# A group norm's last two steps, moved two half steps later in a hand-written order of events

## The reference

```
o   = retention(rotary(q), rotary(k), v)        # 512 x 128 of one head
mu  = mean(o, -1);  var = mean((o - mu)^2, -1)
o_r = (o - mu) * rsqrt(var + 1e-5) * silu(g_r)   # head group norm and gate
```

## Time and profile before

| | |
|---|---|
| median of three runs | 1423.04 us |
| the profiled execution | 1422.83 us, span 1420.7 us |
| PE busy | 1374.6 us, 97% of the span |
| DVE busy | 1037.6 us, 73% |
| ACT busy | 748.3 us, 53% |
| POOL busy | 114.0 us, 8% |
| granted TensorE clock, mean | 0.993 of 2.4 GHz |

### The profile page before, as it was taken

The page is one execution under the profiler, slowest core; times in us unless marked ns, Lnnn a source line. Parts: engine busy times, 40 slices in busy tenths (PEclk is TensorE's granted clock), DMA queues, the critical chain, the costliest instruction groups (busy, mean ns, idle before and its releaser), DMA issues.

```text
span 1420.7 us, 22721 instructions
## 1 busy us (share of the span) xinstructions
PE 1374.6 (97%) x8648; PEld 1230.9 (87%) x8648; DVE 1037.6 (73%) x1115; ACT 748.3 (53%) x1013; POOL 114.0 (8%) x164
## 2 busy tenths in 40 slices
PE   6999999999999999999989999989999999999997
PEld 6999999999787788767768888789999999978786
DVE  6977887788789874657664344687788777779796
ACT  6545544544685552667763323554454445448663
POOL 0000000001420000333220000000000000024100
PEclk9999999999999999999999999999999999999999
DMA  6323332337997655212113345232333233399974
GB/s 200 93 87 118 118 101 76 118 118 207 249 225 253 237 192 133 75 45 60 46 45 88 90 148 177 75 121 75 117 118 104 82 109 118 116 285 210 247 258 142
DMA packets 161638, 194.47 MB, mean 137 GB/s; under 512 B 6064, under 2 KB 116912, under 8 KB 161456
## 3 DMA queue, kind: packets, MB, share of 16 engines
q1 hardware_dynamic: 147808, 166.74, 36.5%
q0 software_dynamic: 13056, 25.17, 9.7%
q10 hardware_dynamic: 720, 1.84, 0.3%
HBM read 187.43 MB, written 6.29 MB: 136 GB/s over the span
## 4 chain that ended last, share of the span: by engine, by line
PE 74%; DVE 10%; DMA 9%; ACT 3%; issue 2%; POOL 2%; SPq 0%; DVEq 0%; ACTq 0%; POOLq 0%
PE ps L700 15%; PE ps L702 15%; PE ps L703 15%; DMA w_raw<-w_ffn_down 5%; PE ps L666 5%; PE ps L668 5%; PE ps L667 5%; DMA d_sum<-w_ffn_down 2%; PE ps L800 2%; PE ps L801 2%; PE ps L802 2%; DVE w_lo L1826 2%; PE ps L673 1%; PE ps L674 1%; PE ps L675 1%
## 5 line engine op out<-in xcount | busy, mean ns | idle before, releaser
L700 PE MATMUL ps<-s_hi,w_hi 128*128 128x256 f32 x960 | 273.0, 284 | 4.8 <-DVE w_lo L1641 4.8
L702 PE MATMUL ps<-s_lo,w_hi 128*128 128x256 f32 x960 | 272.7, 284 | 0.0
L703 PE MATMUL ps<-s_hi,w_lo 128*128 128x256 f32 x960 | 272.7, 284 | 0.0
L700 PE MATMUL ps<-a_hi,w_hi 128*128 128x256 f32 x816 | 233.1, 286 | 3.0 <-DVE a_lo L1596 3.0
L702 PE MATMUL ps<-a_lo,w_hi 128*128 128x256 f32 x816 | 232.5, 285 | 0.0
L703 PE MATMUL ps<-a_hi,w_lo 128*128 128x256 f32 x816 | 232.4, 285 | 0.0
L1173 ACT ACTIVATE w_hi<-w_sum 128x1024 fp32r<-128x1024 f32 x120 | 124.0, 1057 | 174.9 <-DVE w_sum L1668 80.4
L700 PEld LDWEIGHTS ps<-s_hi,w_hi 128*128 128x128 f32 x960 | 185.5, 193 | 5.1 <-DVE w_lo L1641 5.1
L800 PE MATMUL ps<-w_hi,l_hi 128*128 128x512 f32 x448 | 175.9, 393 | 11.9 <-DVE w_lo L1826 11.9
L702 PEld LDWEIGHTS ps<-s_lo,w_hi 128*128 128x128 f32 x960 | 185.5, 193 | 0.0
L703 PEld LDWEIGHTS ps<-s_hi,w_lo 128*128 128x128 f32 x960 | 185.4, 193 | 0.0
(11 more groups left out here) (203 smaller groups left out, 2577.7 us busy)
## 6 DMA issues: line engine op xcount, KB each, us to landing
w_raw<-w_ffn_down SPq DMA_DIRECT2D x80, 512.0 KB, 5.1
w_raw<-w_ffn_gate SPq DMA_DIRECT2D x64, 512.0 KB, 4.8
w_raw<-w_ffn_up SPq DMA_DIRECT2D x64, 512.0 KB, 5.0
d_sum<-w_ffn_down POOLq DMA_DIRECT2D x48, 512.0 KB, 13.1
w_raw<-w_in SPq DMA_DIRECT2D x44, 512.0 KB, 4.0
d_sum<-w_ffn_down SPq DMA_DIRECT2D x16, 512.0 KB, 9.3
x_mid<-x_tok SPq DMA_DIRECT2D x8, 512.0 KB, 4.9
x_tok<-x_mid SPq DMA_DIRECT2D x8, 512.0 KB, 7.3
```

The lines of the kernel that those rows point to most:

```text
L700: pe.matmul(o, wh, hi[:, k, :], start=first and f == 0 and k == 0, stop=False, skip_group_check=True)
L702: pe.matmul(o, wh, lo[:, k, :], start=False, stop=False, skip_group_check=True)
L703: mm = pe.matmul(o, wl, hi[:, k, :], start=False, stop=last and k == KH - 1, skip_group_check=True)
```

## The change

One line: `gn_e` stands at r = 9 instead of 7, `gn_f` at r = 11 instead of 9.

```diff
     per_pair = 12
-    gn_at = {3: "a", 5: "d", 7: "e", 9: "f"}
+    gn_at = {3: "a", 5: "d", 9: "e", 11: "f"}
     groups = []
```

## The result

The changed kernel took 1425.18 us (median of 19 runs, 1422.08 to 1427.71); the kernel before took 1422.10 us in the 19 runs beside it (1420.32 to 1424.22). The ratio is 1.0022, 95% interval 1.0016 to 1.0029: 3.1 us slower, between 2.3 and 4.1. The time lies inside the range on record and 0.5 us over the predicted time. That it comes so near is luck in part: the three runs shown beforehand (1423.04) lay 0.9 us over the median of the many. The difference from before is nearly twice the forecast 1.7 us, and close to what the first rival gave (1.7 + 1.7).

A forecast was written before the change was run, and what follows sets the result against it. PE, busy 97% of the span, was taken to bound the kernel. Gain 0, DVE's queue 1.52 us and POOL 0.14 sum to +1.66 us: 1424.7 us, own range 1424.0 to 1425.4, 8 in 10 1421.4 to 1427.0.

The forecast's parts named there:

- the first rival: The stall in pair 1 brings the granted clock down, +1.7 us more, 1426.4 us; chance 0.17.
- What the change removes: ACT in pair 1: the last attention tile's Exp starts some 2.5 us earlier, but PE had no gap; gain 0.
- The walk through DVE's queue: Pair 1: the reciprocal starts 6.5 us later, DVE's idle cover is used up, sp_lo and PE's matmul come 1.52 us late.
- POOL's share: Pair 1: POOL's masks and two copies fall beside DVE's w_lo and add 0.14 us; by the skill's rule 0.34 us.
- Pairs 2 and 3, the last norm: Pair 2 has 2 us of slack, pair 3 no following attention tile, the last norm's order is unchanged; cost 0.
- The clock: Behind pair 1's new hole of 1.5 to 1.9 us the granted clock most likely stays up; chance of a fall 0.17.
- The third rival: Everything behind 657 us shifts 1.7 us and the clock's dip behind the hole at 720 goes: 1423.0 us; chance 0.08.

The follow-up runs named there:

- the w_lo kernel: The full change, but in pair 1 DVE's weight split w_lo for unit 14 stands behind the softplus split, not ahead of sp_lo; 1424.14 us, ratio 1.0010.
- the kernel with two more products: The full change with two more products (0.72 us each) on DVE behind the reciprocal, in pair 1 alone; 1426.91 us, ratio 1.0034.

## Why the prediction was right in its mechanism and short in its size

**What the change removes: gain 0.** Right. The Exp came early in the change and in the kernel with the root at 8, and neither is faster than before.

**The walk through DVE's queue: 1.52 us, with POOL 1.66.** Right, place and size. PE's sp_lo matmul came 1.65 us late in the first trace. That the queue is the cause is shown by its dose, in the traces: 1.14 us taken out removed the wait for sp_lo, 1.45 us put in cost 1.44 more. That it starts with the Copy ahead of the root was in the walk too, and the root at r = 8, ahead of that Copy, cost nothing.

**POOL's share.** The sum was right, one term not. The w_lo beside POOL's copies took its usual 1.22 us and sp_lo lost 0.08 us (0.57 against 0.49), so 0.14 was too much and the 0.34 us worked out by the Trainium skill's rule was not there. What waited was POOL:

```profile
660.37 1.52 POOL L2146 COPY cum<-sp 128x128 f32<-128x128 f32 x2
```

Two copies that took 0.53 us together in the trace of before took 1.52 here. The first took its usual 0.29 us; the second, begun 0.08 us behind w_lo, took 1.29 and ended 0.16 us behind w_lo's end. The Trainium skill ("SBUF — State Buffer", the two separate sides) has a lock between the two engines that the first to start holds for a whole instruction; for w_lo and the second copy the trace agrees. For the first copy it shows no wait: w_lo began 0.14 us before that copy's end and still took 1.22 us. I had let DVE be the one that waits. The root again started 1.30 us behind the start of its table load (649.38 to 650.68): the further 1.38 us of drain that the Trainium skill has ("ScalarE: Activation LUTs", section on what ACT_TABLE_LOAD costs) were absent in the changed kernel too.

**Pairs 2 and 3, the last norm: 0.** Right: the kernel with all but pair 1 moved is at 1.0002. In pair 2 the sp_lo matmul had no wait.

**The clock: a chance of 0.17 for its fall, and nothing in the sum.** This is the step that failed. The working compared the new hole with two old ones, 1.34 us (clock stayed at 1.00) and 3.04 us (fell), and took the nearer. The nearer row was one execution. In the ten traces here and before that still have the hole of 1.34 us at 622, the clock falls behind it in three (the changed kernel, all but pair 1, and the w_lo kernel) and not in seven; behind the new hole of 1.4 to 2.8 us it falls in four of four. Nor does length alone decide: a hole of 1.66 us near 484 stood in the trace of before itself, with the clock at 1.00 behind it. So the cost of the change is 1.65 + 1.68 us when the clock falls. The mean over the runs agrees: the granted clock averaged over the span was 0.9914 in 19 runs of the change and 0.9927 in 56 runs of before, unrounded 0.0012 less, and 0.0012 of 1425 us is 1.7 us, the loss of about one fall more per execution. The same difference is 1.9 us for the kernel with two more products and 0.9 us for pair 1 alone, so the size of this part is known only roughly. The median's difference of 3.1 us (2.3 to 4.1) agrees with the first rival's 1.66 + 1.7.

**The third rival, a fall given back later,** is not borne out as it stands: the clock fell behind the hole at 720 in every trace of these sets that has it whole. Further on, something is given back in single executions. The trace of before has the clock down for 10.2 us in all between 915 and 965 us; the four traces with the new hole have it down there for 3.4 us or not at all. But so has that of all but pair 1 (3.4 us), without that hole, so these traces can't say that the hole brings it about. This is why single traces mustn't be compared by their ends: the kernel with two more products had the shortest span (1421.1 us) of the first set's traces and the longest median.

**What stays open.** Why a hole of 1.34 us at 622 brings the clock down in three of ten executions, one of 1.39 us or more at 660 in four of four, and one of up to 1.70 us near 484 in none of thirteen. Something beside the length of the hole counts, what PE does around it or when in an execution it falls; no run here separates that. Open too is the gap of up to 1.48 us at the start of the heads stage in some executions.

## What to carry to other kernels

A step moved later in a list that several engines share is free on an engine only as long as that engine reaches its next deadline with idle time to spare; walk that engine's queue from the moved instruction to the next one that the bounding engine needs, with start-to-start times, and look for the event that the moved step now stands behind (here a copy that waits for filling). And price a new hole in TensorE's work above its length, with the fall of the clock as a case of its own: here a microsecond and a half cost three, since the clock fell behind it, while a hole of the same length elsewhere in the same kernel brought no fall. The gain lay where TensorE already waited, in what stands ahead of the instruction that it waits for and in filling dealt to the step with the longest chain.

## What the runs showed of the hardware

- A hole of 1.4 us in TensorE's work near 660 was followed by a fall of the granted clock to 1.2 GHz in three of three traces and cost 1.68 us on top; with 2.84 us of idle time at the same place, in a fourth, the clock fell too and its part was the same 1.68 us (4.77 less 3.09). A hole of 1.13 to 1.70 us near 484 was followed by none in thirteen traces.
- GpSimd was held up by VectorE, not only the other way: two copies that take 0.53 us together took 1.52 us while VectorE subtracted one 128x1024 tile from another in its usual 1.22 us. The first sp_lo subtraction, begun beside the second copy, took 0.08 us more than before (0.37 against 0.29).
- A program whose instructions, order and data are the same in every execution still spreads over 4 us (1420.3 to 1424.2 for the kernel before). Where the clock falls is part of that: the mean granted clock of its executions lay between 0.990 and 0.996, and of two traces of the changed kernel one had a fall near 626 that the other had not.
